# Mixture-of-experts items of 32 token slots instead of 64, on four column groups of the TensorE array

## The reference, cut to what matters

```python
logits = (xf @ w_router + b_router)
top_val, top_idx = lax.top_k(logits, TOP_K)
top_w = jax.nn.softmax(top_val, axis=-1)
...
for e in range(N_EXPERTS):
    hh = xf @ w_expert_in[e] + b_expert_in[e]          # 1024 -> 2048
    gate = jnp.minimum(hh[:, :D_EXPERT], SWIGLU_LIMIT)
    lin = jnp.clip(hh[:, D_EXPERT:], -SWIGLU_LIMIT, SWIGLU_LIMIT)
    act = (lin + 1.0) * gate * jax.nn.sigmoid(SWIGLU_ALPHA * gate)
    y = y + comb[:, e:e + 1] * (act @ w_expert_out[e] + b_expert_out[e])
```

## Time and profile before

| what | us |
|---|---|
| median of 3 runs (1622.11 to 1623.47) | 1622.26 |
| the profiled execution's own time | 1621.45 |
| its span, first to last instruction | 1619.7 |
| TensorE matmuls busy in the span | 1501.3 |
| L919, `hidden`, 2176 matmul records | 530.1 busy |
| L940, `outward`, 1088 matmul records | 242.1 busy |

### The profile page before, as it was taken

How to read it: one execution, slowest core, us unless ns; L and a number is a source line. 1 busy time by engine, 2 the same in 40 slices (tenths; PEclk the granted TensorE clock), 3 DMA queues, 4 the chain that set the end, 5 groups by cost and what they waited for, 6 DMA issues and landing times.

```text
span 1619.7 us, 17964 instructions
## 1 busy us (share of the span) xinstructions
PE 1501.3 (93%) x6938; PEld 738.6 (46%) x6939; DVE 299.6 (19%) x581; ACT 207.6 (13%) x385; POOL 153.5 (9%) x219
## 2 busy tenths in 40 slices
PE   6999999999999899999999998998998998998993
PEld 3777877557877543333333332333333332333331
DVE  1022112333411321212112112112112112112113
ACT  3000222442100110100000000000000000000001
POOL 0230000010530001000000000000000000000000
PEclk9999999999999899999999999999999999999996
DMA  9767534899355455679999999999999999999991
GB/s 366 297 240 287 196 130 177 307 390 346 86 182 208 157 220 195 247 300 423 423 417 425 419 422 421 415 421 425 419 403 420 412 412 421 413 410 425 423 418 59
DMA packets 78618, 533.56 MB, mean 329 GB/s; under 512 B 7562, under 2 KB 8674, under 8 KB 51730
## 3 DMA queue, kind: packets, MB, share of 16 engines
q1 hardware_dynamic: 67330, 503.47, 76.5%
q0 software_dynamic: 10864, 28.72, 5.5%
q10 hardware_dynamic: 391, 0.93, 0.2%
HBM read 507.62 MB, written 30.50 MB: 332 GB/s over the span
## 4 chain that ended last, share of the span: by engine, by line
PE 67%; DMA 28%; DVE 2%; SPq 1%; issue 1%; ACT 0%; DVEq 0%; ACTq 0%; POOL 0%; POOLq 0%
DMA ring<-in_w_expert_in_dram 26%; PE ps L743 16%; PE ps L919 15%; PE ps L940 15%; PE ps L494 3%; PE ps L628 2%; PE ps L836 2%; PE ps L786 2%; PE ps L801 2%; PE ps L794 2%; PE ps L883 2%; PE ps L891 1%; PE ps L541 1%; PE ps L638 1%; PE ps L618 1%; DMA ring<-in_w_ada_dram 1%
## 5 line engine op out<-in xcount | busy, mean ns | idle before, releaser
L919 PE MATMUL ps<-ring,xgT 128*64 128x512 f32 x1632 | 407.6, 646 | 44.2 <-DMA ring<-in_w_expert_in_dram 44.0
L743 PE MATMUL ps<-hT,ring 128*128 128x264 f32 x1152 | 267.7, 390 | 2.1 <-DMA ring<-in_w_in_dram 2.1
L919 PEld LDWEIGHTS ps<-ring,xgT 128*64 128x64 f32 x1632 | 121.4, 148 | 306.9 <-issue 249.2
L743 PEld LDWEIGHTS ps<-hT,ring 128*128 128x128 f32 x1152 | 217.7, 191 | 56.6 <-issue 19.0
L940 PE MATMUL ps<-moe_ring,actT 128*64 128x512 f32 x1088 | 242.1, 598 | 0.2 <-ACT actT L1160 0.2
L940 PEld LDWEIGHTS ps<-moe_ring,actT 128*64 128x64 f32 x1088 | 77.9, 137 | 140.0 <-issue 135.2
L1458 DVE COPY xg<-ps 128x512 f32<-128x512 f32 x35 | 24.2, 692 | 619.0 <-PE ps L883 619.0
L919 PE MATMUL ps<-moe_ring,xgT 128*64 128x512 f32 x544 | 122.5, 592 | 0.0
L883 PE MATMUL ps<-rows,picked 128*64 128x512 f32 (+1 forms) x420 | 101.4, 599 | 1.6 <-ACT x_rows L1144 1.6
L1156 ACT ACTIVATE glu_s<-glu_g 128x512 f32<-128x512 f32 x34 | 21.4, 630 | 448.7 <-DVE glu_g L1470 448.7
L919 PEld LDWEIGHTS ps<-moe_ring,xgT 128*64 128x64 f32 x544 | 39.1, 137 | 77.7 <-issue 77.7
(11 more groups left out here) (265 smaller groups left out, 1079.1 us busy)
## 6 DMA issues: line engine op xcount, KB each, us to landing
ring<-in_w_expert_in_dram SPq DMA_DIRECT2D x96, 2048.0 KB, 16.6
moe_ring<-in_w_expert_out_dram SPq DMA_DIRECT2D x64, 2048.0 KB, 10.8
moe_ring<-in_w_expert_in_dram SPq DMA_DIRECT2D x32, 2048.0 KB, 17.8
ring<-in_w_in_dram SPq DMA_DIRECT2D x18, 2048.0 KB, 11.0
ring<-in_w_ada_dram SPq DMA_DIRECT2D x12, 2048.0 KB, 8.6
ring<-in_state_ret_dram SPq DMA_DIRECT2D x8, 1024.0 KB, 10.4
vslot<-in_state_ret_dram SPq DMA_DIRECT2D x8, 1024.0 KB, 11.9
out_dram<-ring POOLq DMA_DIRECT2D x8, 1024.0 KB, 8.9
```

Of the source, the lines that this page charges most:

```text
L743: mm = nc.tensor.matmul(ps[:, j, 0:T], ring[s][:, k, j * P:(j + 1) * P], hT[:, k, :], start=(k == 0), stop=(k == KC - 1))
L919: mm = nc.tensor.matmul(side(bank, g), xgT[:, 2 * j + a, :], w[:, a, c * COL:(c + 1) * COL], start=False, stop=(j == 3 and a == 1))
```

## The change

SLOTS goes from 64 to 32. The four 512-column blocks of the hidden width now sit on four column groups of 32 in one bank (gate halves on partitions 0 to 63 and linear halves on 64 to 127 of bank 0), the output's 1024 columns and the gathered rows are four quarters of 256 columns, and `moe_rows` is addressed as quarter rows of 1 KB. The element-wise work on the hidden layer covers 64 partitions instead of 128; `xg`, `xgT`, `actT` and `ostage` hold 256 columns instead of 512. The table of items has up to 8 more items for an expert instead of 4 and can hold 65 items.

```diff
-SLOTS = 64
+SLOTS = 32
+SIDES = P // SLOTS
+QUARTER = D // SIDES
+OVERS = 8
...
-    put("slotval", 2 * token - SKIP)
-    put("over", np.tile(SLOTS * np.arange(1, 5), (P, 1)))
+    put("slotval", SIDES * token - SKIP)
+    put("over", np.tile(SLOTS * np.arange(1, OVERS + 1), (P, 1)))
...
-                    for g in range(2):
-                        mm = nc.tensor.matmul(ps[SLOTS * g:SLOTS * (g + 1), 6, :], picked[0:n, t, 0:SLOTS], rows[0:n, t, g * COL:(g + 1) * COL],
+                    for g in range(SIDES):
+                        mm = nc.tensor.matmul(side(6, g)[:, 0:QUARTER], picked[0:n, t, 0:SLOTS], rows[0:n, t, g * QUARTER:(g + 1) * QUARTER],
...
-                for c in range(2):
-                    for a in range(2):
-                        mm = turn(ps[:, 3, (2 * c + a) * P:(2 * c + a + 1) * P], xg[:, 2 * P * c:2 * P * (c + 1)].rearrange("s (p a) -> s a p", a=2)[:, a, :])
+                for a in range(2):
+                    mm = turn(ps[:, 3, a * P:(a + 1) * P], xg[:].rearrange("s (p a) -> s a p", a=2)[:, a, :])
...
-                    for bank in range(2):
-                        for g in range(2):
-                            c = 2 * bank + g
-                            mm = nc.tensor.matmul(side(bank, g), xgT[:, 2 * j + a, :], w[:, a, c * COL:(c + 1) * COL],
-                                                  start=False, stop=(j == 3 and a == 1))
+                    for g in range(SIDES):
+                        mm = nc.tensor.matmul(side(0, g), xgT[:, a, j * SLOTS:(j + 1) * SLOTS], w[:, a, g * COL:(g + 1) * COL],
+                                              start=False, stop=(j == 3 and a == 1))
...
             def turn_hidden(q):
                 pe.wait_ge(act_ready, q + 1)
+                pe.sem_inc(pe_pace, 1)
                 for a in range(4):
-                    mm = turn(ps[:, 4, a * P:(a + 1) * P], act[:].rearrange("s (p a) -> s a p", a=4)[:, a, :])
+                    mm = turn(ps[:, 4, 2 * SLOTS * a:2 * SLOTS * (a + 1)], act[:].rearrange("s (p a) -> s a p", a=4)[:, a, :])
...
-                        for g in range(2):
-                            mm = nc.tensor.matmul(side(2, g), actT[:, 4 * h + a, :], w[:, a, g * COL:(g + 1) * COL],
+                        for g in range(SIDES):
+                            mm = nc.tensor.matmul(side(2, g)[:, 0:QUARTER], actT[:, a, h * SLOTS:(h + 1) * SLOTS], w[:, a, g * QUARTER:(g + 1) * QUARTER],
...
-                ts(glu_g[:], ps[:, 0, :], LIMIT, None, ALU.min).then_inc(glu_ready, 1)
-                ts(glu_l[:], ps[:, 1, :], LIMIT, -LIMIT, ALU.min, ALU.max).then_inc(glu_step, 1)
+                ts(glu_g[:], ps[0:2 * SLOTS, 0, :], LIMIT, None, ALU.min).then_inc(glu_ready, 1)
+                ts(glu_l[:], ps[2 * SLOTS:P, 0, :], LIMIT, -LIMIT, ALU.min, ALU.max).then_inc(glu_step, 1)
...
-            out_halves = moe_rows.rearrange("t (h n) -> (t h) n", h=2)
+            out_halves = moe_rows.rearrange("t (h n) -> (t h) n", h=SIDES)
...
-                                        bounds_check=2 * T - 1, oob_is_err=False, compute_op=ALU.add).then_inc(eo_stored, 16)
+                                        bounds_check=SIDES * T - 1, oob_is_err=False, compute_op=ALU.add).then_inc(eo_stored, 16)
```

More of the change, by code:

```diff
@@ L64 @@
 _at = 0
-for _name, _w in [("ident", P), ("iota", P), ("selc", T), ("iota3", 3 * E), ("slotval", 3), ("over", 4), ("eye96", 36),
+for _name, _w in [("ident", P), ("iota", P), ("selc", T), ("iota3", 3 * E), ("slotval", 3), ("over", 8), ("eye96", 36),
                   ("ones", P), ("upper", P), ("cos", T), ("sin", T), ("decay", HEADS * TP), ("kdecay", 2 * HEADS),
@@ L197, in trunk_kernel @@
         xs = at("xs", [P, KC, T], top[0])
-        xg = new("xg", [P, COL])
-        xgT = new("xgT", [P, KC, SLOTS])
-        actT = new("actT", [P, KC, SLOTS])
+        xg = new("xg", [P, QUARTER])
+        xgT = new("xgT", [P, 2, SIDES * SLOTS])
+        actT = new("actT", [P, 4, 2 * SLOTS])
         onehot = at("onehot", [P, 3, TOPK, E], top[0])
-        act = new("act", [P, COL])
+        act = new("act", [2 * SLOTS, COL])
         product = at("product", [P, 3, TOPK, E], top[0])
[L204 to L207, removed]
+        glu_g = new("glu_g", [2 * SLOTS, COL])
+        glu_l = new("glu_l", [2 * SLOTS, COL])
+        glu_s = new("glu_s", [2 * SLOTS, COL])
+        ostage = new("ostage", [P, QUARTER])
         assert top[0] <= h_at
@@ L216, in trunk_kernel @@
         top[0] = v_at + 12544
-        over_n = new("over_n", [E, 4])
+        over_n = new("over_n", [E, OVERS])
         item_n = new("item_n", [E, 1])
@@ L906, in biases @@
                 pe.wait_ge(hidden_taken, 2 * q + 2)
-                for bank in range(2):
-                    for g in range(2):
-                        c = 2 * bank + g
-                        nc.tensor.matmul(side(bank, g), bias_sel[:], bsplit[:, c * COL:(c + 1) * COL], start=True, stop=False)
+                for g in range(SIDES):
+                    nc.tensor.matmul(side(0, g), bias_sel[:], bsplit[:, g * COL:(g + 1) * COL], start=True, stop=False)
             def hidden(j, e):
@@ L931, in outward @@
                 pe.wait_ge(eo_taken, q + 1)
-                for g in range(2):
-                    nc.tensor.matmul(side(2, g), bias_out[:], bsplit_out[:, g * COL:(g + 1) * COL], start=True, stop=False)
+                for g in range(SIDES):
+                    nc.tensor.matmul(side(2, g)[:, 0:QUARTER], bias_out[:], bsplit_out[:, g * QUARTER:(g + 1) * QUARTER], start=True, stop=False)
                 pe.wait_ge(act_taken, q + 1)
@@ L1151, in take_gathered @@
                 act_e.wait_ge(xg_turned, q + 1)
-                nc.scalar.copy(xgT[:].rearrange("p (g k) s -> p k g s", g=2), ps[:, 3, :].rearrange("p (k g s) -> p k g s", k=4, g=2)).then_inc(xgT_ready, 1)
+                nc.scalar.copy(xgT[:].rearrange("p a s -> p (a s)"), ps[:, 3, 0:2 * P]).then_inc(xgT_ready, 1)
             def squash(q):
```

8 lines of the change are left out of this document (3 added, 5 removed).

## The result

| | us |
|---|---|
| before, median of 4 runs | 1622.18 |
| after, median of 4 runs (1638.56 to 1649.28) | 1646.07 |
| ratio | 1.0148 (95%: 1.0117 to 1.018) |
| the profiled execution after, its own time | 1638.56 |
| its span | 1636.7 |

The changed kernel is slower by 24 us (1.5%, with 1 outside the interval). The forecast was 1623.6, inside a range of 1605 to 1650: the range held and the largest chance, 0.49, was on slower, but the point was 22 us too low. The forecast's own range, 1614 to 1634, did not hold; the wider one holds because it takes in the rivals at 1639 and 1645.

The account below looks back on a forecast made before the run. TensorE was taken to bound early items and the end, expert weights the stretch between. Terms -7.4 + 19.4 - 10.7 = +1.3 on the profiled 1621.45, with the median 0.8 above, gave 1623.6 us; own range 1614 to 1634, with rivals 1605 to 1650.

Parts of the forecast that it names:

- the two regimes: Expert loop before the change: TensorE bounds early items at 27.36 us each; later, expert weights bound at 30.36 per expert.
- the tail: After the last chunk 0 lands: chunk 5 bounds instead of the last item, 27.6 us instead of 38.07; gain 10.7.
- the count of 49 items: Expert loop: routing the inputs gives 34 items with 64 slots and 49 with 32.
- The item's path: TensorE's steps in one item of 32 slots: sum 15.4, plus a wait of 0.5, 15.9 us.
- The outward step: Item's 64 records of 256 columns on TensorE: 3.5 us if streaming bounds, 5.5 if weight loads are not hidden.
- weight loads at 256 columns: Rival, outward and gather: weight loads bind, outward 5.5, gather 2.3, item about 19; near 1670 us, chance 0.07.
- slower rounds of four: Rival, four-column-group matmuls: 16 records take 2.23 us, 2.5 more per item; near 1652, chance 0.07.
- The scatter loop: Outward, copies, scatter landing, next bias cast: 6.2 us plus landing, 13.8 to 17.5; intervals 16.8 each before expert 7.
- The second part: Experts 7 to 31: one-item experts stay at 30.36; stalls at two-item experts 16.0 and rows 3.4, loss 19.4 us.
- the scatter hides: Rival: full items of 1 KB rows land in under 9.7 us, so every item takes 15.9; 1609, chance 0.20.
- A row costs the same at 1 KB: Rival, scatter rows: a 1 KB row costs as much as 2 KB, 15.6 us more; near 1639, chance 0.08.
- The clock falls: Rival, TensorE: gaps lower its clock in each item, 1.4 more, item 18, plus 5 later; near 1645, chance 0.12.

Follow-up runs that it names:

- the scatter loop was cut: The changed kernel with POOL's cast of bias_out placed ahead of the scatter instead of behind its landing: 1606.97 us, 0.9909 of the kernel before.
- second profile of the changed kernel: The changed kernel run once more, unchanged, beside the other kernels on one chip: 1646.31 us.
- outward moved back: The kernel before with the cast of bias_out ahead of the scatter and hidden(1) ahead of outward on TensorE: 1682.55 us (1.0396).

## Why the prediction was right and wrong

- **What bounds the kernel before**, the two regimes and the tail, was read rightly, and the count of 49 items held.
- **The item's path** was right: 15.9 forecast, 16.07 when the scatter loop was cut. The outward step, named as the unknown, took 3.46 against 3.5. The rivals of weight loads at 256 columns and of slower rounds of four are out by the rows of an item after (64 records in 3.46, 16 of hidden in 1.71).
- **The scatter loop**, 6.2 plus the landing, had the right mechanism and the wrong landings. I gave full items of the three-item experts 10.5 by one row; two of the four took 11.4 to 11.6 and two 4.1, with idle queues. Of the seven scatters from expert 3's first item on, until expert 7, all but one (10.5) landed in 11.2 or 11.3, and 6.2 more is the 17.2 to 17.4 that was seen. Intervals were 17.36 on average instead of 16.8, and that the average fits the loop's 17.4 so well is luck: 4.5 us of the 243 came from the lowered clock, and five intervals had no wait for the bias. Two intervals, 20.27 and 19.01, are over the 18 that the prediction named as breaking it. Expert 6's second item began at 813.87, where the terms give 809.5, and the rest of a miss of 6.2 came until expert 8 (857.5 against 819.6 + 30.36 + 1.3 = 851.3).
- **The second part** failed in one step. I let the first item's outward end at 8.6 and the second wait only for chunk 5, and left the scatter loop and the slow outward out. That sized the stalls of the 22 experts at 13.4 (six places at 1.3, two at 2.8), and they were 30.0. With the cast moved, which takes away the wait and many of the slow outwards at once, they were 16.8, near my sum. Two terms went the other way: one-item experts at 29.94 where I kept 30.36 (9.2 less) and the 3.1 for rows, which do not show on top of it. Net 4.3 too low.
- **The tail** failed in its premise that chunk 5 bounds it. Expert 30 has two items, so three scatters stand in a row, and the last outward waits for the third. From expert 30's first item it took 64.8, and I had 59.4. With the loop cut: 59.7. In the second profile of the changed kernel it took 68.1, so the size of this miss is uncertain by some 3.
- The three misses, 6.2, 4.3 and 5.4, are the 15.8 between 1622.75 and the profiled 1638.56. The median lies 7.5 above the profiled execution and not 0.8; that is the part left open above.
- **Of the rivals**, "the scatter hides" is out: a scatter without rows still lands in 10.8. "A row costs the same at 1 KB" is out: it needs about 1.6 us of rows per expert (twice 0.79), and leaving the rows out saved 0.49. "The clock falls" gave 1645, near the result, but by an item of 18 in the first stretch, lengthened each time. There the clock fell at two items of 14, for 4.5 us where the rival had 18. In the second part it had 5, and lowered clock lengthens outwards inside the loop at most of the two-item experts. So this rival is a part of the miss and not all of it. How much the clock costs alone was not isolated: moving the cast removes the waits and most slow outwards together.

## What to carry to other kernels

When items get shorter, look for the cycle that the long item hid: here a wait for a DMA's landing, 11 us of latency, stood ahead of an unrelated small cast on an in-order engine, and moving one statement turned a loss of 24 us into a gain of 13 (1606.97 against 1620.37 of the kernel before, measured beside it). And count the items before and after a tile is halved: the halves are worth having only where rounding up does not multiply them in a stage that is bound by weights anyway.

## What the runs showed of the hardware

- Matmuls on four column groups of 32 take half the time of as many on two groups of 64: 16 records of 512 columns take 1.71 instead of 3.43 us. Rounds of 256 columns keep this: the 64 records of outward take 3.46 us, where its 32 records of 512 columns on two groups took 6.91, so four weight loads per round add nothing.
- An accumulating indirect DMA lands 4.1 us after its issue when the weight queues are idle and mostly 10.4 to 12.2 beside them, with little difference by what it carries: 10.8 with all rows but one skipped. The Trainium skill ("DMA: Bandwidth & Descriptors", "Queues, rings and completion order") says that a DMA engine goes round-robin between its queues, a whole packet at a time; the rise beside busy queues agrees with it, though no run here varied the packets of the weights.
- A DMA share that reads 1.00 does not mean that the weights come at their fastest: the same 12.58 MB took 30.36 us per expert before and 29.94 after. Where buffers came free later still, with outward moved back, they took 32.5, and there the share fell to 0.95.
